# A decoder step on one core: even and odd k tiles of the moving operands at offsets 32 bytes apart, and another order at the start

## What is computed

```python
h = rmsnorm(x); z = h @ w_in                      # 109 blocks of 128 columns: q, k, v of three mixers, gates
o_a = dsa_attention(...); o_b = moba_attention(...); o_c = retention(...)
m = sig(g_a) * (o_a @ w_pa) + sig(g_b) * (o_b @ w_pb) + sig(g_c) * (o_c @ w_pc)
x = x + m @ w_out
h2 = rmsnorm(x)
x = x + (gelu(dwconv(h2 @ ffn_up)) * (h2 @ ffn_gate)) @ ffn_down
```

## Time and profile before

| | |
|---|---|
| median of 3 runs | 2410.08 us |
| the profiled execution's own time | 2412.37 us |
| its span, first to last instruction | 2410.7 us |
| TensorE busy | 2374.0 us, 98% of the span |
| VectorE / ScalarE / GpSimd busy | 59% / 38% / 13% |
| line 779 in the chain that ended last | 86% of the span |
| mean granted clock of TensorE | 0.996 |

### The profile page before, as it was taken

One profiled execution on the slowest core, in us unless ns is written; L12 is line 12 of the kernel. 1 busy time (PEld: TensorE's weight loads), 2 busy tenths in 40 slices (PEclk: granted clock), 3 DMA queues, 4 the chain that ended last, 5 costly groups with the idle time before them and its releaser, 6 DMA issues.

```text
span 2410.7 us, 44511 instructions
## 1 busy us (share of the span) xinstructions
PE 2374.0 (98%) x17200; PEld 2276.8 (94%) x17208; DVE 1410.3 (59%) x2093; ACT 918.4 (38%) x1274; POOL 313.7 (13%) x626
## 2 busy tenths in 40 slices
PE   8999999999999999999999999999999999999997
PEld 7978999999999898888899999999999999999997
DVE  5545568899897445444445645666653446666443
ACT  5334343433434444334333344333333333333332
POOL 1135110000002223332200011000000000000001
PEclk9999999999999999999999999999999999999998
DMA  7447545556558888989675544444445544444553
GB/s 229 146 131 240 177 139 180 181 171 209 196 182 280 293 281 291 301 278 313 230 261 192 189 152 147 148 153 154 149 145 152 152 155 153 154 149 155 146 152 105
DMA packets 174387, 458.69 MB, mean 190 GB/s; under 512 B 24971, under 2 KB 74491, under 8 KB 174049
## 3 DMA queue, kind: packets, MB, share of 16 engines
q1 hardware_dynamic: 141040, 372.31, 47.5%
q0 software_dynamic: 26080, 75.67, 9.7%
q10 hardware_dynamic: 7056, 7.88, 0.9%
HBM read 425.27 MB, written 27.52 MB: 188 GB/s over the span
## 4 chain that ended last, share of the span: by engine, by line
PE 94%; DMA 1%; DVE 1%; ACT 1%; issue 1%; POOLq 0%; DVEq 0%; POOL 0%; SPq 0%; ACTq 0%
PE ps L779 86%; PE ps L1005 1%; PE ps L1046 1%; PE ps L852 1%; ACT w_hi L1087 1%; DMA vpg<-in_cache_a_v 1%; DMA vpg<-in_cache_b_v 1%; PE ps L1028 1%; PE ps L976 0%; DMA xT<-in_x 0%; PE ps L968 0%; PE ps L864 0%; PE ps L919 0%; PE ps L959 0%; PE ps L955 0%
## 5 line engine op out<-in xcount | busy, mean ns | idle before, releaser
L1334 DVE TENSOR_TENSOR w_lo<-w_raw,w_hi 128x1024 fp32r<-128x1024 f32 (+1 forms) x622 | 750.7, 1207 | 798.2 <-ACT w_hi L1087 794.1
L779 PE MATMUL ps<-h_hi,w_hi 128*128 128x320 f32 x3696 | 1148.9, 311 | 12.3 <-DVE w_lo L1334 11.1
L779 PE MATMUL ps<-h_lo,w_hi 128*128 128x320 f32 x3696 | 1140.8, 309 | 0.0
L779 PE MATMUL ps<-h_hi,w_lo 128*128 128x320 f32 x3696 | 1138.8, 308 | 0.0
L1087 ACT ACTIVATE w_hi<-w_raw 128x1024 fp32r<-128x1024 f32 (+1 forms) x622 | 647.5, 1042 | 800.6 <-PE ps L779 782.9
L779 PEld LDWEIGHTS ps<-h_hi,w_hi 128*128 128x128 f32 x3696 | 696.5, 188 | 51.4 <-issue 47.7
L779 PEld LDWEIGHTS ps<-h_hi,w_lo 128*128 128x128 f32 x3696 | 695.8, 188 | 0.0
L779 PEld LDWEIGHTS ps<-h_lo,w_hi 128*128 128x128 f32 x3696 | 693.9, 188 | 0.7
L779 PE MATMUL ps<-y_hi,w_hi 128*128 128x320 f32 x688 | 212.5, 309 | 1.6 <-DVE yt L1406 1.6
L779 PE MATMUL ps<-y_lo,w_hi 128*128 128x320 f32 x688 | 212.2, 309 | 0.0
L779 PE MATMUL ps<-y_hi,w_lo 128*128 128x320 f32 x688 | 210.5, 306 | 0.0
(11 more groups left out here) (320 smaller groups left out, 2068.7 us busy)
## 6 DMA issues: line engine op xcount, KB each, us to landing
w_raw<-in_w_in SPq DMA_DIRECT2D x258, 512.0 KB, 4.9
w_raw<-in_ffn_up SPq DMA_DIRECT2D x86, 512.0 KB, 3.9
w_raw<-in_ffn_gate SPq DMA_DIRECT2D x86, 512.0 KB, 3.7
w_raw<-in_ffn_down SPq DMA_DIRECT2D x80, 448.0 KB, 3.4
kpg<-in_cache_b_k SPq DMA_DIRECT2D x128, 128.0 KB, 4.5
vpg<-in_cache_b_v POOLq DMA_DIRECT2D x128, 128.0 KB, 5.0
kpg<-in_cache_a_k SPq DMA_DIRECT2D x128, 128.0 KB, 4.2
vpg<-in_cache_a_v POOLq DMA_DIRECT2D x128, 128.0 KB, 4.8
```

The source lines that it names most:

```text
L779: mm = mmul(bank[q][:, 0:T], wp[:, s, cols], xp[:, x.k0 + k, :], start=(x.first and k == 0 and t == 0), stop=(x.last and k == x.nk - 1 and ...
L1334: tt(w_lo[:, s, 0:n], w_raw[:, s, 0:n], w_hi[:, s, 0:n].bitcast(F32), ALU.subtract).then_inc(w_lo_done, 1)
```

## The change

1. **Layout.** Every hi and lo tensor is cut into its even and its odd k tiles. Even hi tiles and odd lo tiles lie together; then come 32 bytes; then odd hi tiles and even lo tiles. `tile(x, k)` finds tile k. The offsets modulo 64 in the order of the matmuls are then, for `h`, `oa`: 0, 32, 0 for an even k and 32, 0, 32 for an odd one; for `m`, `y` and `ob`: 32, 0, 32 and 0, 32, 0. Nothing is computed differently. The two instructions that fill `oa` and `ob` on each of ScalarE and VectorE become two each, with half the elements and a stride of two tiles in `ost`.
2. **Order at the start.** The first four jobs (ki, qi0, qi1, qi2) go by turns: their four first halves, then their four second halves. Weights w1, w2 and w3 are transferred ahead of x2 and x3. ScalarE and VectorE prepare units 2 and 3 before they split k tiles 8 to 15. GpSimd's loads wait for x2 in place of x1.
3. **Sum of squares.** VectorE adds the four tiles of squares to one (two more additions, of 640 and of 320 columns), all after unit 4 is prepared, and TensorE sums over partitions with 1 matmul in place of 4.

```diff
+        self.turns = 4 if kind == "ki" else 2 if self.opens else 1
...
-    out = []
-    for job, own in zip(jobs, units):
-        if job.opens:
-            out += [x for two in zip(own, units[own[0].at + 1]) for x in two]
-        elif not (own[0].at and jobs[own[0].at - 1].opens):
-            out += own
+    out, at = [], 0
+    while at < len(jobs):
+        turns = jobs[at].turns
+        out += [x for some in zip(*units[at:at + turns]) for x in some]
+        at += turns
...
-        h_hi = fix("h_hi", [P, KD, T], F32R)
+        half = [P, KD // 2, T]
+        h_hi0, h_lo1 = fix("h_hi0", half, F32R), fix("h_lo1", half, F32R)
         epsc = fix("epsc", [P, 1])
-        h_lo = fix("h_lo", [P, KD, T], F32R)
+        h_hi1, h_lo0 = fix("h_hi1", half, F32R), fix("h_lo0", half, F32R)
+        h_hi, h_lo = (h_hi0, h_hi1), (h_lo0, h_lo1)
+        def tile(x, k):
+            return x[k % 2][:, k // 2, :]
...
-        oa_hi, oa_lo = ro("oa_hi", [P, 8, T], F32R), ro("oa_lo", [P, 8, T], F32R)
+        oa_hi0, oa_lo1 = ro("oa_hi0", [P, 4, T], F32R), ro("oa_lo1", [P, 4, T], F32R)
+        ro("oa_gap", [P, 8])
+        oa_hi1, oa_lo0 = ro("oa_hi1", [P, 4, T], F32R), ro("oa_lo0", [P, 4, T], F32R)
...
+        rm = at(0, 10240), at(10272, 20512), at(ring_at, ring_at + 10240), at(ring_at + 10272, ring_at + 20512)
+        m_hi0, m_hi1, m_lo0, m_lo1 = (r(n, half, F32R) for r, n in zip(rm, ("m_hi0", "m_hi1", "m_lo0", "m_lo1")))
...
-        y_hi = at(0, 28160)("y_hi", [P, KF1, T], F32R)
-        y_lo = at(28192, 56352)("y_lo", [P, KF1, T], F32R)
+        ry, half = at(0, 56352), [P, KF1 // 2, T]
+        y_hi0, y_lo1 = ry("y_hi0", half, F32R), ry("y_lo1", half, F32R)
+        ry("y_gap", [P, 8])
+        y_hi1, y_lo0 = ry("y_hi1", half, F32R), ry("y_lo0", half, F32R)
...
             features(1)
-            transfer(1)
+            for v in range(1, 4):
+                transfer(v)
             features(2)
             features(3)
-            for v in range(2, SP_LEAD):
+            for v in range(4, SP_LEAD):
                 transfer(v)
...
-            pool.wait_ge(x_arrived[1], 16)
+            pool.wait_ge(x_arrived[2], 16)
...
-                            mm = mmul(bank[q][:, 0:T], wp[:, s, cols], xp[:, x.k0 + k, :],
+                            mm = mmul(bank[q][:, 0:T], wp[:, s, cols], tile(xp, x.k0 + k),
...
-            for k in range(4):
-                mm = mmul(bank[2][:, 0:T], ones[:, :], sqx[:, k, :], start=(k == 0), stop=(k == 3))
-            mm.then_inc(n_sum, 1)
+            mmul(bank[2][:, 0:T], ones[:, :], sqx[:, 0, :], start=True, stop=True).then_inc(n_sum, 1)
...
                 if k == 7:
                     high(1)
-            high(2)
+                    high(2)
+                    dense(1)
+            dense(1)
             for g in range(4):
                 ks = slice(4 * g, 4 * g + 4)
                 fn(sqx[:, ks, :], xT[:, ks, :], ACT.Square).then_inc(x_sq, 1)
-            dense(3)
+            dense(2)
             act.wait_ge(n_sum, 1)
             fn(rstd[:, :], bank[2][:, 0:T], ACT.Sqrt, bias=epsc[:, :], scale=1.0 / D).then_inc(n_root, 1)
-            dense(3)
+            dense(2)
...
-                fn((oa_hi, ob_hi)[m][:, :, :], ost[:, m, :, :], ACT.Copy).then_inc(rounded, 1)
+                for i in range(2):
+                    ins = fn((oa_hi, ob_hi)[m][i][:, :, :], ost[:, m, i:8:2, :], ACT.Copy)
+                ins.then_inc(rounded, 1)
...
                 if k == 7:
                     low(1)
-            low(2)
+                    low(2)
+                    dense(1)
+            dense(1)
             for g in range(1, 4):
                 dve.wait_ge(x_sq, g + 1)
-                ins = tt(sqx[:, 0:4, :], sqx[:, 0:4, :], sqx[:, 4 * g:4 * g + 4, :], ALU.add)
-                if g < 3:
-                    V(ins)
-                dense(1)
-            ins.then_inc(x_sqs, 1)
+                V(tt(sqx[:, 0:4, :], sqx[:, 0:4, :], sqx[:, 4 * g:4 * g + 4, :], ALU.add))
+            V(tt(sqx[:, 0:2, :], sqx[:, 0:2, :], sqx[:, 2:4, :], ALU.add))
+            tt(sqx[:, 0, :], sqx[:, 0, :], sqx[:, 1, :], ALU.add).then_inc(x_sqs, 1)
+            dense(2)
             dve.wait_ge(n_root, 1)
             nc.vector.reciprocal(rstd[:, :], rstd[:, :]).then_inc(n_rstd, 1)
-            dense(16)
+            dense(15)
```

More of the change, by code:

```diff
@@ L313, in build @@
         vpg = rg("vpg", [P, V_LOTS, 2, 2, 256])
[L314 to L315 removed]
+        ro = at(ring_at, 109408)
+        oa_hi0, oa_lo1 = ro("oa_hi0", [P, 4, T], F32R), ro("oa_lo1", [P, 4, T], F32R)
+        ro("oa_gap", [P, 8])
+        oa_hi1, oa_lo0 = ro("oa_hi1", [P, 4, T], F32R), ro("oa_lo0", [P, 4, T], F32R)
+        oa_hi, oa_lo = (oa_hi0, oa_hi1), (oa_lo0, oa_lo1)
         misc_at = ro.at - R
[L317 removed]
+        ob_hi0, ob_lo1 = ro("ob_hi0", [P, 4, T], F32R), ro("ob_lo1", [P, 4, T], F32R)
+        ro("ob_gap", [P, 8])
+        ob_hi1, ob_lo0 = ro("ob_hi1", [P, 4, T], F32R), ro("ob_lo0", [P, 4, T], F32R)
+        ob_hi, ob_lo = (ob_hi0, ob_hi1), (ob_lo0, ob_lo1)
         x1_at = ro.at - R
@@ L1095, in evacuated @@
                     act.wait_ge(m_done, job.n + 1)
-                    fn(m_hi[:, job.n, :], m_f[:, job.n, :], ACT.Copy).then_inc(rounded, 1)
+                    fn(tile(m_hi, job.n), m_f[:, job.n, :], ACT.Copy).then_inc(rounded, 1)
                 elif job.kind == "out":
@@ L1100, in evacuated @@
                         act.wait_ge(s_in, 80)
-                    fn(h_hi[:, job.n, :], x1[:, job.n, :], ACT.Copy, scale=gffn[:, job.n:job.n + 1]).then_inc(rounded, 1)
+                    fn(tile(h_hi, job.n), x1[:, job.n, :], ACT.Copy, scale=gffn[:, job.n:job.n + 1]).then_inc(rounded, 1)
                     squares(job.n, job.n)
@@ L1104, in evacuated @@
                     act.wait_ge(bank_free, j + 1)
-                    fn(y_hi[:, job.n % KF1, :], yt[:, job.n % 2, :], ACT.Copy).then_inc(rounded, 1)
+                    fn(tile(y_hi, job.n % KF1), yt[:, job.n % 2, :], ACT.Copy).then_inc(rounded, 1)
                 elif job.kind == "d2":
@@ L1147, in _ @@
                     act.wait_ge(x_arrived[k // 4], 16)
-                fn(h_hi[:, k, :], xT[:, k, :], ACT.Copy, scale=gmix[:, k:k + 1]).then_inc(rounded, 1)
+                fn(tile(h_hi, k), xT[:, k, :], ACT.Copy, scale=gmix[:, k:k + 1]).then_inc(rounded, 1)
                 if k == 2:
@@ L1271, in split_c @@
                 for k in range(KD):
-                    fn(h_hi[:, k, :], oc_f[:, k, :], ACT.Copy).then_inc(rounded, 1)
+                    fn(tile(h_hi, k), oc_f[:, k, :], ACT.Copy).then_inc(rounded, 1)
             def sample(x):
@@ L1385, in evacuate @@
                     dve.wait_ge(rounded, BEFORE["h2"] + n + 1)
-                    stt(h_lo[:, n, :], x1[:, n, :], gffn[:, n:n + 1], h_hi[:, n, :].bitcast(F32), ALU.mult, ALU.subtract)\
+                    stt(tile(h_lo, n), x1[:, n, :], gffn[:, n:n + 1], tile(h_hi, n).bitcast(F32), ALU.mult, ALU.subtract)\
                         .then_inc(split, 1)
@@ L1417, in later @@
                     dve.wait_ge(rounded, BEFORE["m"] + n + 1)
-                    tt(m_lo[:, n, :], m_f[:, n, :], m_hi[:, n, :].bitcast(F32), ALU.subtract).then_inc(split, 1)
+                    tt(tile(m_lo, n), m_f[:, n, :], tile(m_hi, n).bitcast(F32), ALU.subtract).then_inc(split, 1)
                 elif job.kind == "up":
@@ L1439, in later @@
                     i = n % KF1
-                    tt(y_lo[:, i, :], yt[:, n % 2, :], y_hi[:, i, :].bitcast(F32), ALU.subtract).then_inc(split, 1)
+                    tt(tile(y_lo, i), yt[:, n % 2, :], tile(y_hi, i).bitcast(F32), ALU.subtract).then_inc(split, 1)
             def dense(n):
@@ L1483, in _ @@
                 dve.wait_ge(rounded, k + 1)
-                stt(h_lo[:, k, :], xT[:, k, :], gmix[:, k:k + 1], h_hi[:, k, :].bitcast(F32), ALU.mult, ALU.subtract)\
+                stt(tile(h_lo, k), xT[:, k, :], gmix[:, k:k + 1], tile(h_hi, k).bitcast(F32), ALU.mult, ALU.subtract)\
                     .then_inc(split, 1)
@@ L1663, in split_c @@
                     dve.wait_ge(rounded, BEFORE["oc"] + k + 1)
-                    tt(h_lo[:, k, :], oc_f[:, k, :], h_hi[:, k, :].bitcast(F32), ALU.subtract).then_inc(split, 1)
+                    tt(tile(h_lo, k), oc_f[:, k, :], tile(h_hi, k).bitcast(F32), ALU.subtract).then_inc(split, 1)
             def sample(x):
@@ L1725, in _ @@
                 dve.wait_ge(rounded, BEFORE["oab"] + m + 1)
-                tt((oa_lo, ob_lo)[m][:, :, :], ost[:, m, :, :], (oa_hi, ob_hi)[m][:, :, :].bitcast(F32), ALU.subtract)\
-                    .then_inc(split, 1)
+                for i in range(2):
+                    ins = tt((oa_lo, ob_lo)[m][i][:, :, :], ost[:, m, i:8:2, :], (oa_hi, ob_hi)[m][i][:, :, :].bitcast(F32),
+                             ALU.subtract)
+                ins.then_inc(split, 1)
             dense(UNIT_END["up", 0] - at)
```

8 lines of the change are left out of this document (3 added, 5 removed).

## The result

The change makes the kernel slower: a median of 2425.13 us over 4 runs (2424.03 to 2427.12) against 2409.65 us over 4 runs of the kernel before (2408.96 to 2411.55), a ratio of 1.0063 [1.0051, 1.0076], or 15.5 us. Forecast were 2391.0 us and a range of 2379 to 2407. The profiled execution took 2424.12 us, with a span of 2422.4 us against 2410.7 us.

What follows compares the result with a forecast made beforehand. TensorE was taken as the bound, mainly line 779's matmuls. Layout 15.5 + 1.7, less 1.3 for V's waits, plus start 3.4 gave 19.3 us saved, so 2391.0 us; range 2379 to 2407.

Steps and rivals of the forecast that it cites:

- The bound: TensorE, busy 2374.0 of 2410.7 us, mostly line 779; only shorter matmuls there or fewer holes in TensorE can pay.
- Start: TensorE's start: 1.0 us from a hole, 1.6 from the sum over partitions, 0.8 from a later hole; 3.4 us saved.
- Removal of the lower clock stretch: Attention stretch: up to 2 us more if the lower clock goes, named only with the rival of all at the lowest level.
- The fills of oa and ob: ScalarE and VectorE: two more instructions each, of half the size, hidden by the jobs before them; cost 0.
- The layout: Line 779: more changes of offset modulo 64 shorten matmuls; 15.5 us for h, m and y, 1.7 for oa and ob.
- the third change: Line 779, h, m and y: the last unchanged succession becomes a change, taken as one step of 3.33 ns per k tile, 15.5 us.
- 1.7 more for oa and ob: Line 779, 256 k tiles of oa and ob: from no change to three, two steps, 1.7 us saved.
- The step before it: Windows of line 779: w_in on operand h read as 144.1 ns per matmul, from 33 us / 229.
- The loss in V's waits: Attention stretch, 720 to 1240 us: an earlier TensorE waits longer for pages of V, taking 1.3 us off the gain.
- the offset of the operand that is read twice decides: Rival, line 779: x_hi at 32 is slow, now half of all k tiles; 2415 to 2431 us; chance 0.09.
- above 146 for slower: Windows of line 779 in up and gate: above 146 ns per matmul would show the slower rival.
- The layout does nothing: Rival, line 779: 866 ns is a floor or levels have another source; only the start pays, 2406.7 us; chance 0.15.

Runs made afterwards that it cites:

- e1: The kernel before with the change's new start and sum of squares alone, old layout: 2406.57 against 2408.93 us, ratio 0.999.
- e5: e1 with h cut into separate even and odd pieces without the flip, and y moved by 32 bytes: 2409.25 us against 2410.37 for the kernel before.
- e9: e1 with the weights (w_raw, w_hi, w_lo) moved 64 bytes down and all moving operands left in place: 2434.43 us.
- e17: e16 with h's hi and lo exchanged (hi 32, lo 0) and y at hi 0, lo 224, no alternation: 2422.28 us.
- e18: e16 with the change's even-odd flip put on y alone: 2405.36 us.
- e3: The kernel before with h cut and its matmuls reordered so offsets change after every second read: 2412.22 against 2408.93 us, ratio 1.0013.
- e16: e1 with m, oa, ob and y moved to h's distances from w_hi (0 and 32 modulo 256): 2404.35 against 2410.53 us, ratio 0.9979.
- e4: The kernel before with y_lo 32 bytes further, giving y_hi and y_lo equal offsets modulo 64: 2413.22 us.
- e12: e1 with all moving operands but h put at 64 and 96 modulo 128, weights as before: 2412.15 against 2409.2 us, ratio 1.0008.

## Why the prediction was wrong

**The bound** was right: line 779, and matmul time in whole steps. **Start**: right in all three terms; 3.4 us forecast, 3.7 in the profile, 2.4 in e1's medians. Removal of the lower clock stretch was not in the sum. The fills of oa and ob at 0: nothing in the traces speaks against it.

**The layout** is where it failed, at one sentence: "Since times go in whole steps per two tiles, the third change brings none, one or two. I take one". That was 15.5 us saved, with 1.7 more for oa and ob; it was 21.7 us lost and 0. The step rested on "in oa and ob every matmul starts at the same offset modulo 64 as the one before it, and they are the slowest ... so the changes of offset are worth something". The three places also differed in their distance from the weights: x_hi 0 bytes from w_hi in h, 32 in m and y, 64 in oa and ob, modulo 256. I had looked only at moving operands and only modulo 64. Three levels and one explanation that orders them is too little: e5 kept the alternation and lost a level, e9 kept all operands and lost up to three. The step before it, 144.1 ns for w_in, was also too good: w_in before is mixed, 503 pairs at 130 and 197 at 131, 144.8 ns in the mean.

What holds in its place: before, h_hi lies exactly 32,768 bytes behind w_hi, the best place seen, and the change takes every odd tile from (0, 32) to (32, 0). In this order of reads (32, 0) is up to two levels worse even when nothing alternates (e17), and the alternating tensor is at the same 132, not at the mean of both (e18: 132, not 131). That much the runs show. It isn't a rule that a pair takes its worse tile's level: m in the kernel after has even tiles at (32, 64) and odd ones at (64, 96), which alone gave 131 and 132, and is at 131. Nor is (32, 0) bad in every order: in e3 it cost one level at most. The part of the old idea that is left is that equal offsets of hi and lo were at 132 wherever they lay, and that pa rose from there to 130 in e16, the two steps forecast, but at h's place. h had the most to lose: 11.6 + 0.9 + 2.4 + 4.5 of the 21.7 us.

**The loss in V's waits**, 1.3 us, had the right mechanism and the wrong sign, since TensorE came later: 2.1 us of waits in place of 4.5.

**The rivals.** The one on the other side, "the offset of the operand that is read twice decides", gave 2415 to 2431, and the time fell into it, as did "above 146 for slower" in the windows. Its fact, that h has x_hi at 0 and is the only one seen at 144.4, was the right one to look at. Its mechanism holds in part: x_hi at 32 is worse where it is 32 from the weights with x_lo at 0, but x_hi at 32 with x_lo at 64 gives 131, and x_hi at 96 gives 134. The argument against it, "m and y still beat oa and ob, where nothing lies at 32", again counted from the slab's beginning. "The layout does nothing" was the formula's case and is excluded by after against e1, and by e9 and e16.

The Trainium skill (TensorE: Matmul & The Clock Gate, Back-to-back issue gap) has N / 2.4 + 2.5 ns for an isolated matmul, by estimate 135.8 ns for 320 columns. It adds that in a stream of weight loads and matmuls both set the spacing, and that the formula is then too high at large N. Here, in such a stream, the measured 144.4 to 148.9 ns are 8.6 to 13.1 ns above it, and the spread of 4.5 ns between places is more than its fixed 2.5 ns.

**Left open.** Why the first part of up and gate is at 131 and the second at 130, with the same operands at the same addresses, in e16 too, and why the second is at 131 in e4 and e12. When a pair takes the worse tile's level and when not. Why the order of reads changes what (32, 0) costs. Whether w_raw's place has a part in it. What in the chip counts modulo 256. x_hi at a distance of 160, and which tensors neighbouring addresses would favour at other widths, were not tried.

## What to carry to other kernels

When TensorE streams at its limit, an operand's place relative to the weights is a tuning variable. Here what counted fits a period of 256 bytes, so that 1280-byte tiles, a multiple of it, gave a whole tensor one place, and the best place was worth 4.5 ns of 149 per matmul. Move the weights alone and then the operand alone before you explain a level by the order of reads; count matmuls per window in stretches with one operand. And before changing a layout, look which stretch is already at the best level, since it can only lose, and which one waits for another engine, since it can't win.
